# Moving the second layer's modulation products to other blocks of the first layer's MLP

## The reference

```python
for l in range(DEPTH):
    mod = silu(c) @ w_mod[l] + b_mod[l]          # 6 x 1024 values: shift, scale, gate, twice
    modc = silu(c_ctx) @ w_mod[l] + b_mod[l]     # the same for the context tokens
    h = rms_norm(x, g_norm1[l]) * (1 + sc1) + sh1
    ...                                          # mixers, merge, output projection
    x = x + g1 * y
    x = x + g2 * (square(relu((rms_norm(x, g_norm2[l]) * (1 + sc2) + sh2) @ w_ff1[l])) @ w_ff2[l])
    ...                                          # in layer 0 the same for the context tokens
```

## Time and profile before

| | us |
|---|---|
| median of three runs | 2102.94 |
| the profiled execution, its own time | 2108.77 |
| its span, first to last instruction | 2107.0 |
| MLP of layer 0, PE's first block to the barrier | 923 to 1289 |

### The profile page before, as it was taken

One profiled execution on the slowest core, in us unless ns is written; L12 is line 12 of the kernel. 1 busy time (PEld: TensorE's weight loads), 2 busy tenths in 40 slices (PEclk: granted clock), 3 DMA queues, 4 the chain that ended last, 5 costly groups with the idle time before them and its releaser, 6 DMA issues.

```text
span 2107.0 us, 24715 instructions
## 1 busy us (share of the span) xinstructions
PE 1735.9 (82%) x9538; PEld 1458.4 (69%) x9538; DVE 1084.5 (51%) x1895; ACT 728.2 (35%) x1354; POOL 631.5 (30%) x380
## 2 busy tenths in 40 slices
PE   3595768999779998889999995957888678878998
PEld 1383548887467777658888783845877566778998
DVE  6796962244164334256685666155335174445555
ACT  3213324244333433142323223233334434334443
POOL 0441013232112212244455442511511311233443
PEclk8697879999779999989999997988999789988999
DMA  6352212211101123204433544110322212342553
GB/s 250 142 185 81 88 51 85 61 55 52 46 30 53 54 97 106 82 27 171 148 140 120 220 180 159 55 51 11 96 73 72 68 45 64 129 168 102 182 187 130
DMA packets 55846, 216.98 MB, mean 103 GB/s; under 512 B 17313, under 2 KB 17459, under 8 KB 41139
## 3 DMA queue, kind: packets, MB, share of 16 engines
q1 hardware_dynamic: 41232, 202.13, 27.2%
q10 hardware_dynamic: 14499, 13.29, 2.0%
HBM read 210.15 MB, written 5.24 MB: 102 GB/s over the span
## 4 chain that ended last, share of the span: by engine, by line
PE 66%; DVE 18%; ACT 5%; issue 4%; DMA 2%; POOL 2%; ACTq 1%; POOLq 0%; DVEq 0%; SPq 0%
PE bank L1507 35%; PE bank L1549 8%; PE bank L1521 6%; PE bank L1669 3%; DVE mjunk L1015 3%; PE bank L1785 3%; PE bank L1761 2%; PE bank L1531 2%; DVE arena L1041 2%; DVE acc L1015 2%; ACT wH L655 2%; PE bank L1769 1%; PE bank L1567 1%; POOL wL L524 1%; DVE arena L1146 1%
## 5 line engine op out<-in xcount | busy, mean ns | idle before, releaser
L655 ACT ACTIVATE wH<-raw 128x1280 fp32r<-128x1280 f32 (+5 forms) x380 | 295.4, 833 | 632.7 <-PE bank L1507 436.9
L526 POOL TENSOR_TENSOR wL<-raw,wH 128x768 fp32r<-128x768 f32 (+5 forms) x190 | 329.1, 1736 | 511.1 <-ACT wH L655 489.0
L524 POOL TENSOR_TENSOR wL<-raw,wH 128x1280 fp32r<-128x1280 f32 (+5 forms) x98 | 231.8, 2365 | 645.3 <-ACT wH L655 645.3
L1507 PE MATMUL bank<-hH,wH 128*128 128x512 f32 (+1 forms) x976 | 351.4, 360 | 82.5 <-POOL hL L543 51.3
L1507 PE MATMUL bank<-hL,wH 128*128 128x512 f32 (+1 forms) x976 | 344.7, 353 | 0.0
L1507 PE MATMUL bank<-hH,wL 128*128 128x512 f32 (+1 forms) x976 | 343.9, 352 | 0.0
L1507 PEld LDWEIGHTS bank<-hH,wH 128*128 128x128 f32 x976 | 194.5, 199 | 122.9 <-issue 55.9
L1507 PEld LDWEIGHTS bank<-hH,wL 128*128 128x128 f32 x976 | 195.6, 200 | 22.2
L1507 PEld LDWEIGHTS bank<-hL,wH 128*128 128x128 f32 x976 | 195.9, 201 | 20.3
L1507 PE MATMUL bank<-oH,wH 128*128 128x512 f32 (+1 forms) x576 | 195.2, 339 | 7.8 <-POOL wL L526 7.8
L1000 DVE TENSOR_TENSOR wL<-raw,wH 128x1280 fp32r<-128x1280 f32 (+1 forms) x92 | 122.7, 1342 | 147.9 <-ACT wH L655 147.6
(11 more groups left out here) (204 smaller groups left out, 3153.3 us busy)
## 6 DMA issues: line engine op xcount, KB each, us to landing
raw<-in_p_ff SPq DMA_DIRECT2D x64, 1024.0 KB, 4.9
acc<-in_p_mod SPq DMA_DIRECT2D x48, 1024.0 KB, 5.0
raw<-in_p_ml SPq DMA_DIRECT2D x12, 1024.0 KB, 7.5
raw<-in_p_na SPq DMA_DIRECT2D x12, 1024.0 KB, 4.8
raw<-in_p_mga SPq DMA_DIRECT2D x16, 512.0 KB, 3.5
raw<-in_p_mgc SPq DMA_DIRECT2D x16, 512.0 KB, 3.4
raw<-in_p_mgb SPq DMA_DIRECT2D x8, 1024.0 KB, 4.8
raw<-in_p_out SPq DMA_DIRECT2D x8, 1024.0 KB, 5.0
```

The costliest lines, as they stand in the source:

```text
L524: pool.tensor_tensor(l_[:, 0:cut], r_[:, 0:cut], h_[:, 0:cut].bitcast(F32), ALU.subtract)
L526: pool.tensor_tensor(l_[:, cut:k * w], r_[:, cut:k * w], h_[:, cut:k * w].bitcast(F32), ALU.subtract)\
L655: act.activation(flat(wH, n)[:, part], flat(raw, n)[:, part], ACT.Copy)\
L1507: ins = pe.matmul(dst, w_[:, kk, c:c + P], r_[:, kk, lo:TOK], start=kk == k0 and m == 0, stop=kk == k0 + kn - 1 and m == 2)
```

## The change

The function `ff_mods` becomes a table, `FF_MODS`. Each round now has six steps: one in block 1, one in block 4, two in block 5, one in block 6 and one in block 7. SP issues the loads of a block's steps directly behind the load of the same block, not of the next one. On DVE the steps of a block come after `share_ahead` and after `hidden_low`, not before.

```diff
-def ff_mods(j):
-
-    i, q = j // 8, j % 8 - 4
-    if j < 0 or q < 0:
-        return ()
-    return (MODS + 4 * i + q,) if i < 2 else (MODS + 8 * (i - 1) + 2 * q, MODS + 8 * (i - 1) + 2 * q + 1)
+FF_MODS = [[MODS + 6 * (j // 8) + q for q in ((), (0,), (), (), (1,), (2, 3), (4,), (5,))[j % 8]] for j in range(32)]
@@ SP
                     for j, n in enumerate(loads(name, l)):
                         load(n)
                         if (name, l) == ("ff", 0):
-                            for m in ff_mods(j - 1):
+                            for m in FF_MODS[j]:
                                 load_mod(m)
-                    if (name, l) == ("ff", 0):
-                        for m in ff_mods(31):
-                            load_mod(m)
@@ DVE
                         if j >= 4:
                             residual(u, 2 * (j - 4), M_GATE2)
-                        if l == 0:
-                            for m in ff_mods(8 * i + j):
-                                mod(m)
                         share_ahead(n0 + 8 * i + j)
                         if j < 3:
                             hidden_low(u, i, j, 1)
+                        if l == 0:
+                            for m in FF_MODS[8 * i + j]:
+                                mod(m)
```

## The result

The changed kernel takes 2135.17 us (median of four runs, 2132.34 to 2138.35), the kernel before 2103.8 (four runs, 2102.66 to 2108.77): a ratio of 1.0145, 95% interval 1.0122 to 1.0168. It is slower by 31.4 us. The forecast was 46.4 us slower, 2149 us, with a range of 2132 to 2164: the sign and the range hold, the size was too large by half.

What follows compares the result with a forecast made beforehand. PE bounds the phase, waiting only when SP holds a block's load behind a modulation step. Waits 51.4 + restarts 10.0 - old waits 11.4 - end 3.6 = +46.4 us on 2102.94, giving 2149 us, range 2132 to 2164.

Steps and rivals of the forecast that it cites:

- the held load: On SP's queue, the load of block 6 stands behind a step load that waits for DVE's step in block 4.
- the four waits: PE waits before block 6 of each round: 14.8 us in rounds 0 and 1, 10.9 in 2 and 3; 51.4 together.
- the two old ones: PE's waits before blocks 23 and 31, 3.98 and 3.83 us, go with their restarts: 11.4 us gained.
- The issue after the end of block 4: SP issues block 6's load 10.28 us after block 4 ends in rounds 0 and 1, 6.35 in 2 and 3.
- the step in block 5: Its instructions run alone, POOL idle, so block 7's load leaves some 6 us after block 5's end and is hidden.
- The landing: Block 6's load, issued 0.4 us behind a step's load, takes 8.3 us to land.
- Rival 1: Block 6's held load lands in 4.8 us, each wait 3.5 shorter, 14 us less in all: 2135 us; chance 10%.
- From landing to PE: One part of the conversion and both parts of the split take 7.09 us before PE begins the block.
- rival 2: Block 7 is late too, its load waiting for both steps of block 5 beside POOL: 2166 us; chance 5%.
- The clock: After each new wait PE restarts at a lower clock and loses 2.5 us, between 1.7 and 3.2: 10.0 in all.
- The end of the MLP: Layer 1's first load no longer waits for late steps: 5.8 us remain after PE's end, a gain of 3.6.
- The step in block 1: It runs in DVE's idle time after the block's squares, 4.6 us for four instructions, and costs nothing.

Runs made afterwards that it cites:

- Experiments 1 and 4: Both on the changed kernel. 1: SP issues step loads behind the next block's load, 2100.51 us. 4: four buffers instead of two for layer 1's step data, 2086.47 us.
- experiment 9: The changed kernel with the products of the step in block 4 of each round computed twice: 2148.46 us, ratio 1.0213.
- Experiment 2: The changed kernel with the load of each round's step 3 behind the load of block 6 instead of ahead of it: 2127.56 us, ratio 1.011.
- Experiment 3: The changed kernel with one step in each of blocks 1, 2, 4, 5, 6, 7 and SP's step loads one block later: 2099.31 us, ratio 0.9978.

## Why the prediction was right, and where it was off

**The mechanism** was right at each link: the held load, its place, the four waits, the two old ones gone. Experiments 1 and 4 take the hold away in two ways, by order and by buffers, and the loss goes both times; experiment 9 lengthens what is waited for, and the loss grows with it.

**The waits**, forecast at 51.4 us, measured 36.0. The other terms held, so this one makes the difference: 36.0 + 10.0 - 11.4 - 3.3 = 31.3 us, by the same sum. By the terms of the waits:
- The issue after the end of block 4, forecast 10.28 us in rounds 0 and 1 and 6.35 in rounds 2 and 3, was 5.91 (975.57 - 969.66) and 3.62 (1172.94 - 1169.32, where the residual of block 20 began). That is 14.2 us too much in the four rounds, and it is the step of the prediction that failed. I took the row of block 4 of before, where POOL split block 6 beside DVE. But the change is what keeps block 6 from being there to split, so POOL is idle and the step runs alone. The prediction used this very fact for the step in block 5 and missed it for that in block 4. Experiment 2, in which block 6 comes in time, shows the slow step again. This is the residual of block 20:

```profile
1169.32 0.88 DVE L1409 SCALAR_TENSOR_TENSOR arena<-bank,modT,arena 128x256 f32<-128x256 f32 x2 [4.49 <-PE bank L1494]
```

- The landing, forecast 8.3, was 6.9 to 7.0 in each round: 5.5 us too much. Rival 1 priced this at 14 us and gave 2135 as its total, which is the measured time; but by its own mechanism only 5.5 of the 15 us came. The number agrees by chance. The rows that the 8.3 came from were not the only kind of pair. The next one of the same trace (block 9, issued at 995.63) landed in 6.9:

```profile
raw<-in_p_ff SPq DMA_DIRECT2D x1, 1024.0 KB, 6.9
```

- From landing to PE, forecast 7.09, was 7.8 to 8.1 (982.49 to 990.37 in round 0), since DVE's steps of block 5 now run beside POOL's split (3.72 us for the first part, 2.92 in the earlier trace rows): 3.3 us too little. Round 1 of experiment 9, where they don't, has 6.1.
- Block 23 is late by 0.88 us. This is not rival 2, whose load waits for both steps of block 5; it waits for the first alone. It went out at 1186.48, 6.3 us after block 21's end at 1180.20, and landed after 8.7. The prediction tested block 7 for rounds 0 and 1 only, where 12.8 us are allowed; by its own terms rounds 2 and 3 allow 10.9 + 13.4 - 8.3 - 7.09 = 8.9, and the shorter waits left less. Its reason that POOL idles during that step was wrong too: in round 0 the step's fourth instruction ran beside the split of block 6, and the load of block 7 went out 8.6 us after the end of block 5 (989.11 - 980.54), not 6.

These make -14.2 - 5.5 + 3.3 + 0.9 = -15.5, against the 15.4 that are missing.

**The clock.** Four restarts of 2.5 us were forecast, 10.0 in all. Measured by block 6's length less 10.88: 3.1 (990.37 to 1004.40), 2.6, 1.8 (1187.74 to 1200.45) and 2.5 (1285.36 to 1298.74), 10.0 in all. The granted clock shows it in round 0. It is 0.50, the lower level of 1.2 GHz, for the first 6 us of the block, and then 1.00 (windows: stretch, length, busy of PE, PEld, DVE, ACT, POOL, clock, DMA):

```profile
993.40:996.40 3.00, 3.00 (x8) 2.33 (x8) 1.45 (x4) 0.39 (x1) 0.00 (x0) 0.50 0.79 294
996.40:999.40 3.00, 3.00 (x14) 2.46 (x14) 0.44 (x2) 1.62 (x2) 2.04 (x1) 1.00 1.05 370
```

The blocks end where these residuals begin:

```profile
1004.40 0.88 DVE L1409 SCALAR_TENSOR_TENSOR arena<-bank,modT,arena 128x256 f32<-128x256 f32 x2 [4.56 <-PE bank L1494]
...
1200.45 0.88 DVE L1409 SCALAR_TENSOR_TENSOR arena<-bank,modT,arena 128x256 f32<-128x256 f32 x2 [4.56 <-PE bank L1494]
...
1298.74 0.88 DVE L1409 SCALAR_TENSOR_TENSOR arena<-bank,modT,arena 128x256 f32<-128x256 f32 x2 [4.57 <-PE bank L1494]
```

**The end of the MLP.** Forecast 5.8 us from PE's end to the barrier and a gain of 3.6; PE's wait to the norm's first matmul fell from 11.74 to 8.41, a gain of 3.3. DVE's wait for the conversion of 8.70 us is 0.49:

```profile
1300.10 1.49 DVE L987 TENSOR_TENSOR wL<-raw,wH 128x1280 fp32r<-128x1280 f32 x1 [0.49 <-ACT wH L642]
```

**The step in block 1** cost nothing, as forecast: in the window PE has no wait over 0.3 us in blocks 0 to 5 of any round. But the margin is thin. Experiment 3 adds one more such step, in block 2, and PE waits 3.8 us.

## What to carry to other kernels

In a queue that issues in program order, look at every load for the slowest wait that stands ahead of it, not for its own: here a transfer that nobody needed soon held one that PE needed, and issuing the loads of low-priority data one block earlier in the queue, with nothing else changed, cost 43.6 us (experiment 5). Place such a load behind the loads that are due before its wait can end, or give it buffers enough that it doesn't wait. And when a wait is added, price the links of its chain in the new situation. An engine that starves because of it stops slowing the others, so durations from the busy steady state can be too long; an engine that catches up behind it can slow them.

## What the runs showed of the hardware

The second of two 1 MB loads issued 0.4 us apart landed after 6.9 us (975.57 in the changed kernel, 995.63 in the kernel before), after 8.3 (984.75 in the kernel before, 1284.10 in the changed one) or after 8.7 (1186.48 in the changed kernel), and the first after 4.7 to 5.0 each time. Both values are in both kernels, so the change does not choose between them; what does was not tested and stays open.

A DVE instruction on 128x1024 took 1.22 us while POOL was idle and 3.96 and 2.85 beside POOL's split; POOL's first part took 2.88 alone and 3.4 to 3.9 beside such instructions.

The restart of PE after a wait cost 1.8 to 3.1 us for waits of 7.6 to 10.1 us, with no clear order by length (7.58 us cost 1.8, 7.57 cost 2.5), and no more for the waits of 10.1 to 15.0 us of experiment 9 (2.0 to 2.2, by the same reading).
